# The last two units of a token-major matrix run tile by tile, with plain transposes, the next unit in token halves, and weight remainders in pieces

## The reference, cut to what matters

```python
for l in range(2):
    h = rms_norm(x, g_pre_mix[l])
    x = x + rms_norm(hybrid_mixer(h, ...), g_post_mix[l])   # ends in y @ w_out
    h = rms_norm(x, g_pre_ffn[l])
    x = x + rms_norm(conv_ffn(h, ...), g_post_ffn[l])       # ends in a @ w_down
# then, with weights of their own
x = x + 0.5 * _rmsnorm(_swiglu(_rmsnorm(x, ffn1_pre_g)), ffn1_post_g)
h = _rmsnorm(x, mix_pre_g)                                  # two attentions, merged, @ w_out
x = x + _rmsnorm(merged @ w_out, mix_post_g)
x = x + 0.5 * _rmsnorm(_swiglu(_rmsnorm(x, ffn2_pre_g)), ffn2_post_g)
```

## Time and profile before

| what | value |
|---|---|
| median of 3 runs | 2925.21 us |
| span of the profiled execution | 2926.2 us |
| PE busy | 2831.4 us, 97% |
| DVE, ACT, POOL busy | 42%, 44%, 40% |
| mean granted TensorE clock | 0.989 of full |
| chain that ended last | PE 80%, ACT 5%, DVE 4%, Pool 2% |

### The profile page before, as it was taken

The page is one execution under the profiler, slowest core; times in us unless marked ns, Lnnn a source line. Parts: engine busy times, 40 slices in busy tenths (PEclk is TensorE's granted clock), DMA queues, the critical chain, the costliest instruction groups (busy, mean ns, idle before and its releaser), DMA issues.

```text
span 2926.2 us, 43251 instructions
## 1 busy us (share of the span) xinstructions
PE 2831.4 (97%) x15918; PEld 2340.0 (80%) x15918; DVE 1231.3 (42%) x2141; ACT 1302.1 (44%) x1999; POOL 1168.2 (40%) x368
## 2 busy tenths in 40 slices
PE   7999999999999999999999999999998999999999
PEld 6765688888888765788888879998896678889987
DVE  7164212555222364114555067770204531277731
ACT  5356434554335356335545254452415353444442
POOL 3300355444454100554444454454531325544453
PEclk9999999999999899999999999999999999999999
DMA  6200133233224100332332323323330213323332
GB/s 171 83 12 12 54 100 114 87 100 100 101 87 118 51 12 12 86 116 86 100 94 96 100 88 101 103 101 112 107 94 16 76 35 101 120 73 101 103 111 79
DMA packets 326468, 249.91 MB, mean 85 GB/s; under 512 B 36727, under 2 KB 294471, under 8 KB 326343
## 3 DMA queue, kind: packets, MB, share of 16 engines
q1 hardware_dynamic: 323864, 246.85, 27.2%
q10 hardware_dynamic: 2478, 1.39, 0.2%
HBM read 245.74 MB, written 2.70 MB: 85 GB/s over the span
## 4 chain that ended last, share of the span: by engine, by line
PE 80%; issue 6%; ACT 5%; DVE 4%; DVEq 2%; POOL 2%; ACTq 1%; DMA 0%; SPq 0%; POOLq 0%
PE pair L1863 62%; PE pair L2229 8%; PE pair L2071 2%; PE pair L2107 1%; PE pair L2090 1%; POOL wlo L553 1%; DVE wlo L1542 1%; PE pair L2153 1%; PE pair L2151 1%; PE pair L2139 1%; PE pair L2169 1%; ACT tmp L655 1%; ACT whi L921 0%; DVEq L1528 0%; ACT bP L1033 0%
## 5 line engine op out<-in xcount | busy, mean ns | idle before, releaser
L553 POOL TENSOR_TENSOR wlo<-raw,whi 128x2048 fp32r<-128x2048 f32 x195 | 906.8, 4650 | 1505.9 <-ACT whi L619 1505.9
L1863 PE MATMUL pair<-hh,whi 128*128 128x512 f32 x1600 | 630.2, 394 | 9.2 <-DVE hl L1183 7.2
L1863 PE MATMUL pair<-hl,whi 128*128 128x512 f32 x1600 | 626.3, 391 | 0.0
L1863 PE MATMUL pair<-hh,wlo 128*128 128x512 f32 x1600 | 626.0, 391 | 0.0
L619 ACT ACTIVATE whi<-raw 128x2048 fp32r<-128x2048 f32 x195 | 373.0, 1913 | 562.2 <-PE pair L1863 550.3
L1863 PEld LDWEIGHTS pair<-hh,whi 128*128 128x128 f32 x1600 | 302.7, 189 | 76.8 <-issue 12.4
L1863 PEld LDWEIGHTS pair<-hh,wlo 128*128 128x128 f32 x1600 | 302.5, 189 | 63.7
L1863 PEld LDWEIGHTS pair<-hl,whi 128*128 128x128 f32 x1600 | 302.6, 189 | 61.3
L2229 PE MATMUL pair<-hh,whi 128*128 128x256 f32 x640 | 185.0, 289 | 8.1 <-POOL wlo L584 6.1
L1191 DVE SCALAR_TENSOR_TENSOR pair<-pair,gp_d 128x512 f32<-128x512 f32 x32 | 22.3, 698 | 388.6 <-ACT sq L627 388.3
L2229 PE MATMUL pair<-hl,whi 128*128 128x256 f32 x640 | 181.2, 283 | 0.0
(11 more groups left out here) (350 smaller groups left out, 5314.6 us busy)
## 6 DMA issues: line engine op xcount, KB each, us to landing
raw<-in_w_in SPq DMA_DIRECT2D x118, 512.0 KB, 3.8
raw<-in_w_up SPq DMA_DIRECT2D x88, 512.0 KB, 4.2
raw<-in_ffn_w_gate SPq DMA_DIRECT2D x44, 512.0 KB, 4.0
raw<-in_ffn_w_up SPq DMA_DIRECT2D x44, 512.0 KB, 4.3
raw<-in_w_down SPq DMA_DIRECT2D x40, 512.0 KB, 3.9
raw<-in_ffn_w_down SPq DMA_DIRECT2D x40, 512.0 KB, 3.9
raw<-in_w_out SPq DMA_DIRECT2D x24, 512.0 KB, 4.1
raw<-in_w_proj_nsa SPq DMA_DIRECT2D x16, 256.0 KB, 3.8
```

The source lines that it names most:

```text
L553: pool.tensor_tensor(wlo[:, s, :], raw[:, s, :], whi[:, s, :].bitcast(f32), ALU.subtract).then_inc(lo_ready, 1)
L1863: o = pe.matmul(out, l, r, start=start and first, stop=stop and last)
```

## The change

- by_tokens on PE: all units but the last two run as before. The last two run together, token tile by token tile, so that the four tiles end a quarter of two units apart. For this their weights have homes of their own (X_O, Y_O and so on), in activation tiles that are free by then; ACT and Pool fill them (spare_upper, spare_rest), and the first two units of the next stage are copied earlier (next_upper), Pool taking the second one in 8 pieces of 256 columns (rest_in_pieces).
- scaled moves from Pool to DVE and takes the root with it: xg = x * root * gain. The diagonal goes; PE transposes against the identity. The turns of tiles 0 and 1 stand inside tile 3 of the projection, those of tiles 2 and 3 inside the next stage's first unit.
- That first unit runs in token halves (first_in_halves): 2 x 48 matmuls of 256 columns.
- xg has two buffers in place of three. The second half of the gain behind the down projection has a copy of its own (gp1), since gp_d lies where hl is written.
- Two further edits: the value-and-gate units are copied and subtracted over 1120 columns (valued_upper, valued_rest), and three units in each layer and two in the second block have their remainder in pieces.

```diff
+def rest_in_pieces(u):                                   # Pool
+    v, s = u // 2, u % 2
+    pool.wait_ge(hi_ready, u + 1)
+    for c in range(0, 2048, PIECE):
+        o = pool.tensor_tensor(wlo[:, s, c:c + PIECE], raw[:, s, c:c + PIECE], whi[:, s, c:c + PIECE].bitcast(f32), ALU.subtract)
+    o.then_inc(lo_ready, 1)
...
+def layer_rest(u0, first, end):                          # Pool, units of one layer
+    rest_of(first, u0 + 4)
+    valued_rest(u0 + 4)
+    valued_rest(u0 + 5)
+    rest_of(u0 + 6, u0 + 11)
+    for u in range(u0 + 11, u0 + 14):
+        rest_in_pieces(u)
+    rest_of(u0 + 14, end)
...
 # ACT, by_tokens, after the squares of the first column half
+next_upper(u + 2 * n, u + 2 * n - 3)
 post_root(vv, s, b, 0, s0)
+pre_root(m, 0)
 post_root(vv, s, b, 1, s0)
-pre_root(m, 0)
+next_upper(u + 2 * n + 1, u + 2 * n - 2)
+pre_root(m, 1)
 post_root(vv, s, b, 2, s0)
-pre_root(m, 1)
+pre_upper(m, 0, s0)
+pre_root(m, 2)
+pre_upper(m, 1, s0)
 post_root(vv, s, b, 3, s0)
-pre_root(m, 2)
-pre_upper(m, 0, s0)
 pre_root(m, 3)
-pre_upper(m, 1, s0)
 pre_upper(m, 2, s0)
 pre_upper(m, 3, s0)
-upper(vv + 1, s)
...
 # DVE, by_tokens
+def scaled(i):
+    dve.drain()
+    if i == 0:
+        dve.wait_ge(S.gq_in, 16 * (m + 1))
+    dve.wait_ge(S.root2_done, 4 * m + i + 1)
+    if i >= XH:
+        dve.wait_ge(S.turned, 8 * m + 2 * (i - XH) + 2)
+    for h in range(CH):
+        cols = slice(h * 512, (h + 1) * 512)
+        dve.scalar_tensor_tensor(xg[:, i % XH, cols], x[:, i, cols], root2[:, i:i + 1], gq[:, cols], ALU.mult, ALU.mult).then_inc(S.xg_ready, 1)
+updated(0)
+scaled(0)
+updated(1)
+scaled(1)
+updated(2)
+lower(m, 0, s0)
+lower(m, 1, s0)
+updated(3)
+scaled(2)
+scaled(3)
+lower(m, 2, s0)
+lower(m, 3, s0)
...
 # PE, by_tokens: the last two units
+for i in range(TT):
+    if i == 3 and xg is not None:
+        turn(b + 1, xg, s0, 0)
+    for j in range(2):
+        if i == 0:
+            opened(*at_unit(v, s0, 2 * n - 2 + j))
+        if i == 3 and j == 1 and xg is not None:
+            turn(b + 1, xg, s0, 1)
+        k0, k1 = parts[n - 2 + j]
+        for k in range(k0, k1):
+            wt = [w[:, (k - k0) * 512:(k - k0 + 1) * 512] for w in spares[j]]
+            o = three(bank[4 + held(s0, i)][:, :], wt, [t[:, k, i * P:(i + 1) * P] for t in inp], k == 0, k == parts[-1][1] - 1, swap=True)
...
+def first_in_halves(v, s, m, xg):
+    opened(v, s)
+    for q in range(2):
+        for k in range(KT):
+            if k % 4 == 0:
+                pe.wait_ge(S.h_ready, 8 * m + 4 * q + 3 + k // 4)
+            if q == 0 and k == 4:
+                turn(m, xg, s, 2)
+            for c in range(2):
+                wt = [w[s][:, k * 256 + c * P:k * 256 + c * P + P] for w in (wh, wl)]
+                o = three(bank[2 * s + c][:, 256 * q:256 * q + 256], wt, [t[:, k, 256 * q:256 * q + 256] for t in H], k == 0, k == KT - 1)
...
+        if q == 0:
+            turn(m, xg, s, 3)
```

More of the change, by code:

```diff
@@ L560, in rest_of @@
             def rest_of(first, end):
-                if first % 2:
+                if first % 2 and first < end:
                     rest(first // 2, 1)
@@ L600, in _ @@
             first_rest()
[L601 to L604, removed]
+            for m, (end, x_spare, y_spare) in enumerate(ends):
+                first = ends[m - 1][0] + 2 if m else 1
                 if m in (4, 6):
[L606 to L609, removed]
+                    sums_rest(first - 2 - u2, m // 2 - 2)
+                    first += PU
+                if m in (0, 2):
+                    layer_rest(UL * (m // 2), first, end - 2)
+                elif m == 5:
+                    rest_of(first, u2 + 44)
+                    rest_in_pieces(u2 + 44)
+                    rest_of(u2 + 45, u2 + 50)
+                    rest_in_pieces(u2 + 50)
+                    rest_of(u2 + 51, end - 2)
+                else:
+                    rest_of(first, end - 2)
+                spare_rest(end - 2, x_spare)
+                spare_rest(end - 1, y_spare)
+                if end < UNITS:
+                    rest(end // 2, end % 2)
+                    rest_in_pieces(end + 1)
@@ L677, in by_tokens @@
                             square(b, 0, i, s0)
[L678 removed]
+                    if j <= 2 * n - 5:
                         upper(vv + 1, s)
+                    if j == 2 * n - 5:
+                        spare_upper(u + 2 * n - 2, u + 2 * n - 4, x_spare)
+                    if j == 2 * n - 4:
+                        spare_upper(u + 2 * n - 1, u + 2 * n - 3, y_spare)
+                if n == len(OUT_PARTS):
+                    vv, s = at_unit(v, s0, n - 1)
+                    for i in range(TT):
+                        act.drain()
+                        token_done(vv, s, b, 0, i)
+                        square(b, 0, i, s0)
+                vv, s = at_unit(v, s0, 2 * n - 1)
                 m = b + 1
@@ L1209, in by_tokens @@
                     added(i)
-                    if i > 0 and not last:
-                        diagonal(m, i - 1)
-                if not last:
-                    lower(m, 0, s0)
-                    diagonal(m, 3)
-                    for i in range(1, TT):
-                        lower(m, i, s0)
+                updated(0)
[10 more added lines that the diff above has]
+                lower(m, 3, s0)
             def merged(v, s, yn, hi, lo, gab, first=None):
@@ L1929, in h_tiles, with by_tokens @@
                 return ready
-            def by_tokens(v, s0, parts, b, inp, ready):
+            def by_tokens(v, s0, parts, b, inp, ready, spares, xg=None):
                 n = len(parts)
-                for j in range(2 * n):
+                for j in range(2 * n - 2):
                     c, (k0, k1) = j // n, parts[j % n]
@@ L1950, in by_tokens @@
                             o.then_inc(S.tok_done, 1)
-            def turn(m, xg, s0):
                 for i in range(TT):
-                    pe.wait_ge(S.diag_set, 4 * (m - 1) + i + 1)
-                    for h in range(CH):
-                        pe.wait_ge(S.xg_ready, 8 * m + 2 * i + h + 1)
-                        for k in range(4):
-                            at = h * 512 + k * P
-                            o = pe.matmul(bank[4 * h + held(s0, i)][:, k * P:(k + 1) * P], xg[:, i % XG, at:at + P], diag[:, i % 2], start=True, stop=True)
-                        o.then_inc(S.turned, 1)
+                    if i == 3 and xg is not None:
+                        turn(b + 1, xg, s0, 0)
@@ new lines, in by_tokens, with turn @@
+                    if i < TT - 1:
+                        o.then_inc(S.tok_done, 1)
+                    else:
+                        o.then_inc(tile_done, 4)
+            def turn(m, xg, s0, i):
+                for h in range(CH):
+                    pe.wait_ge(S.xg_ready, 8 * m + 2 * i + h + 1)
+                    for k in range(4):
+                        at = h * 512 + k * P
+                        o = pe.transpose(bank[4 * h + held(s0, i)][:, k * P:(k + 1) * P], xg[:, i % XH, at:at + P], ident)
+                    o.then_inc(S.turned, 1)
```

163 lines of the change are left out of this document (101 added, 62 removed).

## The result

The changed kernel takes 2885.53 us (median of 4 runs, 2883.55 to 2891.07) against 2925.49 us for the kernel before on the same chip: ratio 0.9867, 95% interval 0.9852 to 0.9881, 40 us faster. The forecast was 2901.6 us with a range of 2889 to 2914. The way was right and the size was not: 23.6 us forecast, 40 found.

What follows compares the result with a forecast made beforehand. PE, busy 97%, was taken as the bound. Junctions 9.5, value units 5.4 and remainders in pieces 8.7 sum to 23.6 us, so 2925.2 becomes 2901.6 us; 8 in 10: 2889 to 2914.

Steps and rivals of the forecast that it cites:

- Remainders in pieces: Attention stages: cutting six whole Pool remainders into 256-column pieces shortens PE's waits by 8.7 us, bounds 0 and 14.
- the first paragraph's premise: Whole kernel: PE is busy 97% of 2926.2 us, so only its idle time and removable matmul time are worth anything.
- the leftover collisions: Attention stages: DVE instructions still meeting Pool's pieces were taken to cost 1.1 us for each of six remainders.
- Rival B: Attention pieces only spread the waits and give nothing; gain 15 us, 2910 us; chance 0.20.
- rival A: Everything pays in full: junctions 13, value units 6, pieces 14; 33 us gained, 2892 us; chance 0.18.
- Junctions: Six places where one stage's result becomes the next's input: 9.5 us gained; bounds 13 and -2.
- two of them hardly pay: Junctions into the paired stages, bounded by a chain over ACT, DVE and Pool: 0.1 us gained and 1.4 lost.
- The choice on DVE beside Pool: Junctions: two scaling instructions on DVE were assumed to lose 1.1 us beside Pool's pieces.
- Rival C: Junctions: tile 0's scaling queues behind Pool's whole first-unit remainder, sliding up to 4.5 us at six junctions; 2937 us; chance 0.05.
- Value units: Two value units, in each of two layers: copies and remainders over 1120 of 2048 columns gain 5.4 us; 3 to 6.
- A piece of 256 columns: Pool's remainder pieces: one piece of 256 columns was estimated to take about 0.7 us.
- Rival D: Whole kernel: attention and junction chains take back what single waits give; no change, 2922 to 2927 us; chance 0.05.

## Why the prediction was wrong

- **The failed step is "Remainders in pieces", 8.7 us with bounds 0 and 14.** It priced PE's waits at their own length alone, and its upper bound of 14 was a bound on the waits. Behind it stands the first paragraph's premise that only PE's idle time and matmul time that can go are worth anything: PE at half clock counts as busy there. The pieces gave 22.1 us alone and 21.1 as the last part. In the waits they gave 12.2 us instead of 8.7 (the leftover collisions were overrated: the leftover waits of nP are at most 0.8 us). The other half is not in the step at all: the lower clock level behind each long wait, 15.4 us in before. It could be read in the trace of before: a mean granted clock of 0.989 over the span, PEclk of 0.50 behind the wait, and four transposes at 1.05 us where the same four take 0.60 elsewhere. Rival B, in which the pieces give nothing, is refuted by their 22.1 us and by nP; rival A was nearest, and its 14 us came from the same bound.
- **Junctions, 9.5 us: right in size, in part by luck.** 8.8 us alone, 9.2 in the traces, place by place. That two of them hardly pay was right as well, with the hsum wait where it was forecast. But the trace has new low stretches behind three of the waits there, which the forecast did not have: 3.06 us behind 3.16 us for hsum, 1.71 behind 2.67 for hsum in the second paired stage, 1.70 behind 1.81 for hl into the dilated attention. The first cost nothing in the kernel with pieces of 128 (above); for the other two that was not tried.
- **The choice on DVE beside Pool: right, a little high.** 0.5 to 1.0 us for two scalings against 1.1. Rival C did not happen for the reason given against it: at the junction shown the first unit's whole remainder ends at 829.87, and the scaling of tile 0 starts at 833.55. What C feared, a scaling held by a whole remainder, is real for tile 1 and the second unit: with that remainder whole the kernel is 12.6 us slower over the six junctions, low clock included.
- **Value units, 5.4 us: inside the interval of 7.3.** ACT's copy took 1.14 us and Pool's remainder 2.60 to 2.94, against 1.05 and 2.48; PE's wait is 0.2 us a layer.
- **A piece of 256 columns, 0.7 us as an estimate:** 6.50 us for eight with two of them colliding.
- **Rival D** (no change) is refuted.

## What to carry over

A wait of a busy TensorE has to be priced with what comes behind it: read the granted clock and the duration of a repeated instruction in the few microseconds after the wait, and add what they are short of full clock. Here that doubled the worth of six waits of 2.3 to 5.2 us. If such a wait can't be removed, filling it with unused matmuls gave most of the second half back, as long as TensorE itself was what the next stage waited for.

## What the runs showed of the hardware

- The granted clock fell during a long wait or some time behind it, and came back by itself under full load. Behind the 2.77 us wait PE ran on for some 1.3 us and then at 1.2 GHz until about 157.5; behind bP's 5.2 us wait it was at 1.2 GHz from its first matmul. Sixteen waits of 0.75 us brought no fall, sixteen of 7.8 us brought one each, worth 2.2 us on the mean. (The Trainium skill, "TensorE: Matmul & The Clock Gate", section "HAM oscillation — how this bites in real kernels", describes a wait for data of some 3 to 5 us behind which the next matmuls run at the low clock, every time. The waits of 5.2 and 3.6 us for bP and aP agree; the four for nP, of 2.3 to 2.8 us, are shorter than those on the page and brought a fall too.)
- A wait of a given length does not bring a fall every time. Past the first 30 us, the traces of the 13 kernels (before, changed and eleven experiments) together have 52 waits of PE between 2.3 and 3.2 us, and a low stretch began in or within 2 us behind 50 of them; of 35 waits between 1.75 and 2.05 us it was 14. In before the same wait of 2.05 us in the two paired stages was followed by a low stretch in the first (1757.23) and by none in the second (2602.59).
- Low stretches also come without a wait ahead of them, and not just anywhere. In layer 0 before has one between 126 and 134 us that costs 3.4 us while PE is busy all through. It begins inside 64 small matmuls of 31 columns:

```profile
123.50 5.36 PE L2046 MATMUL pair<-kcT,nqT 64*128 64x31 f32 x64
```
```profile
126.00:130.00 4.00, 4.00 (x32) 3.74 (x32) 1.10 (x2) 0.82 (x1) 4.00 (x1) 0.58 0.00 0
130.00:134.00 4.00, 4.00 (x12) 3.15 (x11) 2.73 (x4) 1.03 (x1) 0.13 (x1) 0.56 0.68 191
```

The same 64 stand in both layers of all 13 traced kernels, 26 times; 19 times the clock fell 2.6 to 5.1 us after the first of them started, and 7 times it did not (in the changed kernel's layer 0, where they take 4.39 us, among others).
- The spread between runs of one kernel follows the granted clock. In the 37 runs of before beside the experiments, those with a mean granted clock of 0.990 took 2920.8 to 2923.3 us, with 0.989 2923.6 to 2926.2, with 0.988 2926.2 to 2929.7, with 0.987 2929.7 to 2931.2. A step of 0.001 over 2925 us is 2.9 us, the distance of these groups.
- A Pool instruction loses as well when it meets DVE: of the eight pieces of the junction two take 1.2 us and six 0.73.
